# A two-block transformer kernel: the differential stage's first two key units from rows that are not yet scaled, the next two tile by tile, and the weight splits ahead of the rotary operations

## The chip, the cores and the metric

The kernel runs on one core of a Trainium2 chip. The time is the device time of the whole program in microseconds (us), as the median of several runs. The engines of a core work side by side, each through its own queue in order: TensorE (PE in the profile) multiplies, VectorE (DVE), ScalarE (ACT) and GpSimd (POOL) work element by element, SyncE (SP) issues the loads. They wait for one another through semaphores.

## What is computed

Two transformer blocks run over 256 rows of width 1024. The part that matters here is the entry of the second layer of the first block, the differential attention, which needs the keys of the 256 latent rows and of the 256 context rows, and the queries and values of the latent (values also of the context) rows:

```python
def rms_norm(x, gain):
    y = x * lax.rsqrt(jnp.mean(x * x, axis=-1, keepdims=True) + EPS)
    return y * gain
...
h_lat = modulate(rms_norm(x, norm_gain[i, 0]), sh1, sc1)        # h * (1 + scale) + shift
h_ctx = modulate(rms_norm(ctx, norm_gain[i, 0]), csh1, csc1)
...
q, k, v = jnp.split(h @ w_in, 3, axis=-1)
q = rms_norm(q.reshape(b, l, DIFF_HEADS, 2, DIFF_HEAD_DIM), q_gain)
k = rms_norm(k.reshape(b, l, DIFF_HEADS, 2, DIFF_HEAD_DIM), k_gain)
...
q_l = apply_rope(q_l, cos, sin)
k_l = apply_rope(k_l, cos, sin)
```

With g = norm_gain * (1 + scale), a row of h is r * (x * g) + shift, where r is one number for each row (the root of the mean square, inverted). So h @ w is r * ((x * g) @ w) + shift @ w. Before this stage `x` and `ctx` get their last part from the feed-forward layer: x = x + g2 * swiglu(...).

## The kernel before

Everything is held transposed: 128 features on the partitions, rows (512 = 256 latent + 256 context) along the free axis, and a row vector of 1024 features is eight tiles k = 0..7. Each product in 32-bit precision is made of three matmuls (`product`, L514): both operands are split into a rounded half (`wh`, `hh`) and a rest (`wl`, `hl`). ScalarE rounds (`round_half`, L491), VectorE subtracts (`split_low`, L498). Weights come in slabs of two halves; four split halves are held at a time, so half q+4 is rounded and split once half q has been used.

The feed-forward output (`ffn_out`, L2757 on TensorE, L2003 on ScalarE, L2344 on VectorE) ends with eight output tiles in the eight banks of PSUM. VectorE adds each to `x_lat` and `x_ctx` (L2306), ScalarE squares them (`norm_square`, L632), GpSimd adds the first six squares (`squares_added`, L749), and TensorE sums over the features with matrices of ones (`norm_sum`, L758 and L763). Meanwhile TensorE runs 3 and later 9 matmuls that nobody reads (`stay_awake`, L2538). ScalarE makes r from the sum (`norm_rstd`, L642 and L645). Then the rows are scaled tile by tile: VectorE multiplies (L709), ScalarE adds the shift and rounds (L685), VectorE makes the rest (L725); `norm_dve` (L697) and `norm_round` (L675) hold these loops.

`DIFF_UNITS` (L780) lists the stage's work for TensorE: eight key units of 512 columns (one for each pair of 64-wide heads), then four times two query units of 256 columns and four value units ("token"). `units_pe` (L1023) takes the first two units tile by tile as the rows come (each `s_h`), and then one unit after the other. Two places after a head unit (lag 2) follows its `unit_sum` (L986, L987). ScalarE (`units_act`, L1051) squares the unit (L997, L999), makes the inverse root (L1008, L1010) and rounds the next weight half. VectorE (`units_dve`, L1093) scales the unit (L1109, which also frees its bank), turns it (rotary operations, L1124 to L1127), and after these splits the next weight half (L1131).

## Time and profile before

| | |
|---|---|
| median of 3 runs | 1194.3 us (1194.27 to 1195.29) |
| the profiled execution | 1192.11 us, its span 1190.4 us |
| PE busy | 1152.2 us, 97% |
| DVE busy | 732.6 us, 62% |
| ACT busy | 556.2 us, 47% |
| POOL busy | 131.0 us, 11% |
| granted TensorE clock, mean | 0.995 |

The span runs from the first to the last instruction; the time holds about 1.7 us more. A busy PE says little by itself here: the matmuls that keep it awake count as busy, and a matmul's duration overlaps its neighbours', so the distance between the starts of two matmuls is what one costs.

### The profile page before, as it was taken

The page shows a single profiled execution, that of the slowest core. Times are in us where ns is not written, and L with a number is a line of the kernel's source. Part 1 is how long each engine was busy: PE and PEld are TensorE (multiplying, and loading weights), DVE is VectorE, ACT ScalarE, POOL GpSimd, SP SyncE. Part 2 cuts the span into 40 slices and gives each one's busy share as a digit, 9 for nine tenths or more (in the row PEclk, how much of TensorE's full clock was granted, in tenths as well). Part 3 has the DMA queues.
Part 4 walks back from the last instruction along what each step waited for, and adds up shares of the span by engine and source line. Part 5 has one row for each costly group of instructions (what it writes and reads, how often), then busy time and mean ns, then how long its engine had stood idle before and what let it go on. Part 6 is the DMA issues. An engine that isn't in the chain of part 4 may idle for free.

```text
span 1190.4 us, 18791 instructions
## 1 busy us (share of the span) xinstructions
PE 1152.2 (97%) x7072; PEld 963.6 (81%) x7072; DVE 732.6 (62%) x1219; ACT 556.2 (47%) x1058; POOL 131.0 (11%) x185
## 2 busy tenths in 40 slices
PE   8999999999999999999998999999998999999998
PEld 6665787787878888778995799999998986799666
DVE  6764576766723333668769696445568585445773
ACT  4344322222223223455447674444566676467662
POOL 0012011122200000221100110000010010132410
PEclk8999999999999999999999999999999999999999
DMA  8999355578722233122340156555544453164210
GB/s 308 379 338 320 113 168 186 187 246 281 248 98 95 83 106 103 39 91 86 112 138 1 37 177 203 186 176 177 179 150 129 137 160 97 51 202 142 109 72 35
DMA packets 121672, 182.85 MB, mean 154 GB/s; under 512 B 4497, under 2 KB 92896, under 8 KB 121600
## 3 DMA queue, kind: packets, MB, share of 16 engines
q1 hardware_dynamic: 113888, 154.44, 38.9%
q0 software_dynamic: 7712, 27.43, 7.0%
q8 instruction: 47, 0.77, 0.3%
q14 instruction: 25, 0.20, 0.1%
HBM read 180.48 MB, written 1.05 MB: 152 GB/s over the span
## 4 chain that ended last, share of the span: by engine, by line
PE 81%; DVE 9%; ACT 5%; issue 3%; POOL 1%; DVEq 0%; ACTq 0%; POOLq 0%
PE ps L516 20%; PE ps L518 20%; PE ps L517 20%; PE ps L947 2%; DVE wl L498 2%; PE ps L948 2%; PE ps L949 2%; ACT wh L491 1%; PE ps L2563 1%; DVE hl L725 1%; DVE nrm L709 1%; PE ps L2930 1%; PE ps L2932 1%; PE ps L2931 1%; PE ps L1199 1%
## 5 line engine op out<-in xcount | busy, mean ns | idle before, releaser
L498 DVE TENSOR_TENSOR wl<-raw,wh 128x1024 fp32r<-128x1024 f32 (+1 forms) x246 | 297.5, 1214 | 225.7 <-ACT wh L491 222.6
L516 PE MATMUL ps<-hh,wh 128*128 128x256 f32 (+3 forms) x1272 | 418.1, 329 | 7.5 <-DVE hl L725 2.8
L517 PE MATMUL ps<-hl,wh 128*128 128x256 f32 (+3 forms) x1272 | 414.0, 325 | 0.0
L518 PE MATMUL ps<-hh,wl 128*128 128x256 f32 (+3 forms) x1272 | 413.2, 325 | 0.0
L491 ACT ACTIVATE wh<-raw 128x1024 fp32r<-128x1024 f32 (+1 forms) x246 | 252.5, 1032 | 261.1 <-PE ps L518 249.6
L516 PEld LDWEIGHTS ps<-hh,wh 128*128 128x128 f32 x1272 | 239.6, 188 | 47.8 <-issue 14.9
L518 PEld LDWEIGHTS ps<-hh,wl 128*128 128x128 f32 x1272 | 240.0, 189 | 20.9
L517 PEld LDWEIGHTS ps<-hl,wh 128*128 128x128 f32 x1272 | 239.0, 188 | 20.3
L516 PE MATMUL ps<-ah,wh 128*128 128x256 f32 (+2 forms) x376 | 126.1, 335 | 2.7 <-DVE big L1109 1.5
L517 PE MATMUL ps<-al,wh 128*128 128x256 f32 (+2 forms) x376 | 124.2, 330 | 0.0
L518 PE MATMUL ps<-ah,wl 128*128 128x256 f32 (+2 forms) x376 | 124.2, 330 | 0.0
L516 PEld LDWEIGHTS ps<-ah,wh 128*128 128x128 f32 x376 | 70.6, 188 | 11.6 <-DVE big L1109 1.7
L518 PEld LDWEIGHTS ps<-ah,wl 128*128 128x128 f32 x376 | 70.6, 188 | 7.3
L517 PEld LDWEIGHTS ps<-al,wh 128*128 128x128 f32 x376 | 70.8, 188 | 7.1
L2332 DVE TENSOR_TENSOR al<-big,ah 128x512 fp32r<-128x512 f32 (+1 forms) x42 | 23.3, 558 | 81.3 <-ACT ah L1995 81.3
L1995 ACT ACTIVATE ah<-big 128x512 fp32r (+3 forms) x42 | 21.8, 524 | 103.4 <-PE ps L518 103.4
L947 PE MATMUL ps<-wh,hh 128*128 128x256 f32 x192 | 54.8, 286 | 3.2 <-DVE wl L498 1.6
L949 PE MATMUL ps<-wh,hl 128*128 128x256 f32 x192 | 53.9, 281 | 0.0
L948 PE MATMUL ps<-wl,hh 128*128 128x256 f32 x192 | 53.9, 281 | 0.0
L749 POOL TENSOR_TENSOR big<-sq 128x512 f32<-128x512 f32 (+2 forms) x4 | 4.4, 1100 | 441.3 <-ACT sq L632 441.3
L1079 POOL TENSOR_TENSOR al<-sq,ah 128x256 fp32r<-128x256 f32 (+2 forms) x32 | 30.7, 960 | 143.7 <-ACT ah L999 143.7
L1109 DVE SCALAR_TENSOR_TENSOR big<-ps,par,rstd 128x256 f32<-128x256 f32 (+3 forms) x60 | 22.6, 404 | 34.0 <-ACT rstd L1010 33.9
(290 smaller groups left out, 1513.3 us busy)
## 6 DMA issues: line engine op xcount, KB each, us to landing
raw<-in_ffn_w_in SPq DMA_DIRECT2D x44, 1024.0 KB, 5.1
raw<-in_ffn_w_out SPq DMA_DIRECT2D x22, 1024.0 KB, 4.9
raw<-in_w_in SPq DMA_DIRECT2D x22, 1024.0 KB, 5.4
big<-in_w_ada SPq DMA_DIRECT2D x16, 1024.0 KB, 10.5
big<-in_w_ada POOLq DMA_DIRECT2D x24, 512.0 KB, 4.5
ex<-in_w_ada POOLq DMA_DIRECT2D x24, 512.0 KB, 5.1
raw<-in_diff_w_in SPq DMA_DIRECT2D x12, 1024.0 KB, 5.1
raw<-in_w_out SPq DMA_DIRECT2D x8, 1024.0 KB, 4.9
```

Of the source, the lines that this page charges most:

```text
L491: ins = nc.scalar.activation(place(wh), v, ACT.Copy)
L498: ins = nc.vector.tensor_tensor(place(wl), v, place(wh).bitcast(F32), ALU.subtract)
L516: nc.tensor.matmul(o, w_hi, m_hi, start=first, stop=False, **kw)
L517: nc.tensor.matmul(o, w_hi, m_lo, start=False, stop=False, **kw)
L518: return nc.tensor.matmul(o, w_lo, m_hi, start=False, stop=last, **kw)
L947: nc.tensor.matmul(oo, mh[:, k, tok], cols(wh), start=first, stop=False)
L948: nc.tensor.matmul(oo, mh[:, k, tok], cols(wl), start=False, stop=False)
L949: ins = nc.tensor.matmul(oo, ml[:, k, tok], cols(wh), start=False, stop=last)
L1079: nc.gpsimd.tensor_tensor(al[:, h % 2, 0:w], sq[:, h % 2, 0:w], ah[:, h % 2, 0:w].bitcast(F32), ALU.subtract).then_inc(s_ulow, 1)
L1109: ins = nc.vector.scalar_tensor_tensor(out=dst, in0=o[:, a:b], scalar=par_of(u["gain"])[0:m, :], in1=inverse_of(u)[:, a:b], op0=ALU.mult, ...
L1995: nc.scalar.activation(ah[:, at % 2, 0:n], big[:, bass.ds(k * n, n)], ACT.Copy)\
L2332: nc.vector.tensor_tensor(al[:, at % 2, 0:n], big[:, bass.ds(k * n, n)], ah[:, at % 2, 0:n].bitcast(F32), ALU.subtract).then_inc(s_as, 1)
```

## The change

ScalarE and VectorE round and split x * g of each tile (without r) into new tiles `eh` and `el` as soon as the tile is updated, beside the squares. They lie in `big`, which now has a fixed place; behind each part stand two columns with the shift. TensorE starts the first two key units on these tiles right after the feed-forward output, in four banks (256 rows and 2 columns of the shift each), with the sum of the squares behind tile 4; the matmuls that nobody reads fall away here. VectorE scales the two units by r inside the loop over the normed tiles (`first_key_scaled` at k = 3 and 5), ScalarE adds shift @ w and squares them (`first_key_square` at k = 5 and 7). Key units 2 and 3 now take the normed rows tile by tile. Two weight halves are split ahead of r instead of one. The banks of the stage rotate through 5, 6, 0, 1, 2, 3, and the head sums stand in banks 4 and 7. In `units_dve` the weight split stands between the scaling of a unit and its rotary operations.

```diff
+        def key_rows_round(act, k):
+            act.wait_ge(s_x, X_OF["diff"] + k + 1)
+            for x, c, at, w in KEY_PARTS:
+                if k == 0:
+                    nc.scalar.activation(eh[:, :, at + w:at + w + 2], key_shift(c), ACT.Copy)
+                ins = nc.scalar.activation(eh[:, k, at:at + w], x[:, k, :], ACT.Copy, scale=gsc[:, 1, 0, k, c:c + 1])
+            ins.then_inc(s_eh, 1)
+        def key_rows_split(dve, k):
+            dve.wait_ge(s_eh, k + 1)
+            for x, c, at, w in KEY_PARTS:
+                if k == 0:
+                    nc.vector.tensor_tensor(el[:, :, at + w:at + w + 2], key_shift(c),
+                                            eh[:, :, at + w:at + w + 2].bitcast(F32), ALU.subtract)
+                ins = nc.vector.scalar_tensor_tensor(out=el[:, k, at:at + w], in0=x[:, k, :],
+                                                     scalar=gsc[:, 1, 0, k, c:c + 1],
+                                                     in1=eh[:, k, at:at + w].bitcast(F32), op0=ALU.mult,
+                                                     op1=ALU.subtract)
+            ins.then_inc(s_el, 1)
+        def first_key_scaled(dve, j):
+            u = DIFF_UNITS[j]
+            b = u["bank"]
+            unit_done(dve, u)
+            nc.vector.tensor_copy(sml[:, 8 + 2 * j:10 + 2 * j], ps[:, b:b + 2, L:L + 1])
+            for c in range(2):
+                ins = nc.vector.tensor_tensor(first_key(j)[:, c * L:(c + 1) * L], ps[:, b + c, 0:L],
+                                              rstd[:, 0, c * L:(c + 1) * L], ALU.mult)
+            ins.then_inc(s_kt, 1)
+        def first_key_square(act, link, j):
+            act.wait_ge(s_kt, j + 1)
+            for c in range(2):
+                part = first_key(j)[:, c * L:(c + 1) * L]
+                ins = nc.scalar.activation(part, part, ACT.Identity, bias=first_key_bias(j, c))
+            link(ins)
+            nc.scalar.activation(sq[:, j, 0:NT], first_key(j), ACT.Square)
+            nc.scalar.activation(ah[:, j, 0:NT], first_key(j), ACT.Square).then_inc(s_usq, 1)
...
@@ units_dve @@
                     ins.then_inc(s_unrm, 1)
+                if halves and not (i < len(phase) and "early" in phase[i]):
+                    for q in halves_after(phase, i):
+                        split_next(dve, q)
                 if i >= lag and phase[i - lag].get("rope"):
...
-                for q in halves_after(phase, i) if halves else ():
-                    split_next(dve, q)
@@ ffn_out, ScalarE @@
+            def first_keys(k):
+                if k == 5:
+                    first_key_square(act, link, 0)
+                elif k == 6:
+                    unit_done(act, DIFF_UNITS[0])
+                    round_next(act, DIFF_UNITS[0]["q"])
+                elif k == 7:
+                    first_key_square(act, link, 1)
...
+                    else:
+                        key_rows_round(act, m)
                     norm_square(act, norm, m)
-                round_next(act, q0 + 20, 2 if layer == 1 else 1)
+                round_next(act, q0 + 20, 2)
@@ ffn_out, VectorE @@
+            def first_keys(k):
+                if k in (3, 5):
+                    first_key_scaled(dve, (k - 3) // 2)
...
+                    elif layer == 0 and m in (1, 3, 5):
+                        key_rows_split(dve, m // 2)
                 if layer == 0:
-                    split_next(dve, q0 + 20)
+                    for m in range(3, KD):
+                        key_rows_split(dve, m)
+                    split_next(dve, q0 + 20, 2)
                     dve.wait_ge(s_x, X_FFN0 + KD)
-                    norm_dve(dve, norm)
-                    split_next(dve, q0 + 21)
+                    norm_dve(dve, norm, first_keys)
+                    split_next(dve, DIFF_UNITS[0]["q"], 2)
@@ TensorE @@
-                if layer == 0:
-                    pe.wait_ge(s_x, X_OF[norm] + 2)
-                    stay_awake(awake[0], 1, tab, 2 * P)
-                    for k in range(N_ADDED - 1, KD):
-                        norm_sum(pe, norm, k)
-                    stay_awake(awake[1], 7, tab, 2 * P)
...
-            units_pe(pe, DIFF_UNITS[:-1], BASE["diff"])
+            for u in DIFF_UNITS[:2]:
+                unit_start(pe, u, True)
+            for k in range(KD):
+                pe.wait_ge(s_el, k + 1)
+                for u in DIFF_UNITS[:2]:
+                    for _, c, at, w in KEY_PARTS:
+                        n = slice(at, at + w + 2)
+                        ins = product(ps[:, u["bank"] + c, 0:w + 2], tile_of(wh, u["q"], KD, P)[:, k, :],
+                                      tile_of(wl, u["q"], KD, P)[:, k, :], eh[:, k, n], el[:, k, n], k == 0,
+                                      k == KD - 1)
+                    if k == KD - 1:
+                        ins.then_inc(used, 1)
+                if k == 4:
+                    for j in range(N_ADDED - 1, KD):
+                        norm_sum(pe, "diff", j)
+            for u in DIFF_UNITS[2:4]:
+                unit_start(pe, u, True)
+            for k in range(KD):
+                pe.wait_ge(s_h, BASE["diff"] + k + 1)
+                for u in DIFF_UNITS[2:4]:
+                    unit_tile(u, k)
+            units_pe(pe, DIFF_UNITS[:-1], before=4)
```

## Rows read from the trace of the kernel before

**Rows 1.** The page's part 4, the chain that ended last, by engine.
```profile
PE 81%; DVE 9%; ACT 5%; issue 3%; POOL 1%; DVEq 0%; ACTq 0%; POOLq 0%
```

**Rows 2.** Timeline of TensorE, 490 to 502 us: start, duration, what, [idle before, releaser].
```profile
490.68 0.39 PE L518 MATMUL ps<-hh,wl 128*128 128x512 f32 x1
492.84 1.10 PE L758 MATMUL ps<-big,tab 128*128 128x512 f32 x2 [0.48 <-POOL big L749]
493.77 1.88 PE L763 MATMUL ps<-sq,tab 128*128 128x512 f32 x4
495.49 4.05 PE L2538 MATMUL ps<-tab 128*128 128x256 f32 x18
500.08 0.47 PE L516 MATMUL ps<-hh,wh 128*128 128x512 f32 x1 [0.54 <-DVE hl L725]
```

**Rows 3.** The same timeline: the first matmuls of units 2, 3 and 4.
```profile
513.13 0.39 PE L516 MATMUL ps<-hh,wh 128*128 128x512 f32 x1
...
519.16 0.39 PE L516 MATMUL ps<-hh,wh 128*128 128x512 f32 x1
...
525.19 0.39 PE L516 MATMUL ps<-hh,wh 128*128 128x512 f32 x1
```

**Rows 4.** Timelines of ScalarE, VectorE and GpSimd, 483 to 512 us.
```profile
487.12 5.58 POOL L749 TENSOR_TENSOR big<-big,sq 128x512 f32<-128x512 f32 x4 [0.90 <-ACT sq L632]
491.10 0.48 DVE L2306 SCALAR_TENSOR_TENSOR x_lat<-ps,ada,x_lat 128x256 f32<-128x256 f32 x1 [0.49 <-PE ps L518]
495.69 0.69 ACT L642 ACTIVATE rstd<-ps,eps_c 128x512 f32<-128x512 f32 x1 [1.24 <-PE ps L763]
497.13 0.48 DVE L709 SCALAR_TENSOR_TENSOR nrm<-x_lat,gsc,rstd 128x256 f32<-128x256 f32 x1 [1.42 <-ACT rstd L645]
499.05 0.88 DVE L725 SCALAR_TENSOR_TENSOR hl<-nrm,ada,hh 128x256 fp32r<-128x256 f32 x2 [0.25 <-ACT hh L685]
500.77 0.87 DVE L725 SCALAR_TENSOR_TENSOR hl<-nrm,ada,hh 128x256 fp32r<-128x256 f32 x2
500.89 0.91 ACT L685 ACTIVATE hh<-nrm,ada 128x256 fp32r<-128x256 f32 x2 [1.14 <-DVE nrm L709]
```

**Rows 5.** Timelines, the later feed-forward entry (680 to 716 us) and one unit's square.
```profile
696.63 0.28 PE L516 MATMUL ps<-hh,wh 128*128 128x258 f32 x1
...
699.03 0.28 PE L518 MATMUL ps<-hh,wl 128*128 128x258 f32 x1
690.20 0.51 ACT L553 ACTIVATE hh<-x_lat,gsc 128x256 fp32r<-128x256 f32 x1 [0.65 <-DVE x_lat L2306]
690.62 0.40 ACT L632 ACTIVATE sq<-x_lat 128x256 f32<-128x256 f32 x1
...
692.61 0.51 ACT L553 ACTIVATE hh<-x_lat,gsc 128x256 fp32r<-128x256 f32 x1 [0.64 <-DVE x_lat L2306]
693.63 0.95 DVE L563 SCALAR_TENSOR_TENSOR hl<-x_lat,gsc,hh 128x256 fp32r<-128x256 f32 x1
698.43 0.47 DVE L563 SCALAR_TENSOR_TENSOR hl<-x_lat,gsc,hh 128x256 fp32r<-128x256 f32 x1
715.40 0.75 DVE L2472 TENSOR_TENSOR ex<-ps,rstd 128x256 f32<-128x256 f32 x2
512.63 0.60 ACT L997 ACTIVATE sq<-ps 128x512 f32<-128x512 f32 x1 [1.35 <-PE ps L518]
```

**Rows 6.** Timelines around the first value unit and the second slab of values.
```profile
551.82 1.04 ACT L491 ACTIVATE wh<-raw 128x1024 fp32r<-128x1024 f32 x1
555.93 1.22 DVE L498 TENSOR_TENSOR wl<-raw,wh 128x1024 fp32r<-128x1024 f32 x1
557.21 0.39 PE L947 MATMUL ps<-wh,hh 128*128 128x256 f32 x1 [1.10 <-DVE wl L498]
```

**Rows 7.** Two-us windows at 1106 and 1110 us: busy time by engine; the number behind POOL is the granted clock.
```profile
1106.00:1108.00 2.00, 0.97 (x9) 0.57 (x7) 0.23 (x2) 1.19 (x3) 0.00 (x0) 1.00 0.00 0
1110.00:1112.00 2.00, 2.00 (x15) 1.10 (x8) 1.62 (x9) 1.34 (x7) 1.79 (x5) 0.50 0.18 45
```

48 lines of the change are left out of this document (37 added, 11 removed).

## The prediction

> **What bounds the kernel now.** I read the page's shares first, then the chain of waits, then the timeline of each engine through the stage. The chain that ended last lies on TensorE for 81% [rows 1], so a change pays where TensorE has no useful matmul, and only there. The timeline of TensorE shows such a place: the last product of the feed-forward output starts at 490.68 and gives way 0.23 us later, and the first product of the keys starts at 500.08. Between them stand only the sum over the squares (L758 and L763, 492.84 to 495.65) and matmuls that nobody reads [rows 2]. The first two key units then follow the normed rows. VectorE makes one tile in 1.72 us (499.05 to 500.77) [rows 4], while six matmuls cost TensorE 1.39 us: a unit's 24 and a head sum's 2 take 513.13 to 519.16, 0.232 us each [rows 3]. The first pair lasts from 500.08 to 513.13, 13.05 us for 11.1 us of matmuls. Unit 4, the first that both kernels run alike, starts at 525.19 [rows 3]. Its start is my yardstick: behind it TensorE runs closed up until 555.9.
>
> **Part 1: the first pair without the row scale.** It removes the gap and the pacing of the pair. A unit of 512 columns becomes twice 258 columns: the 20 steps from 696.63 to 699.03 take 0.12 us each [rows 5], 12 matmuls in a tile 1.44 us, eight tiles 11.5 us. The sum over the squares stands behind tile 4 and costs what it did, 2.8 us [rows 2], now on TensorE's path. If its operands are there, TensorE runs closed up from 490.9 to 490.9 + 11.5 + 2.8 = 505.2.
>
> Are they there? VectorE adds two tiles (four operations at 0.40, the distance between the L2306 starts) and then splits one, later one after the other; a split is two operations at 0.40 to 0.88 [rows 4, 5]. The last add needs the feed-forward output's last product, as it does now (491.10 [rows 4]). Walking both queues through, with 0.42 us for each of a tile's two roundings (690.20 to 690.62 [rows 5]) and 0.32 for each of its two squares on ScalarE (0.40 long, overlapping as the rounding does), and the upper price wherever GpSimd adds, tile 2 is split at 492.0 (TensorE wants it at 493.8), tile 3 at 494.9 (wanted 495.2), tile 4 at 495.7 (wanted 496.7), tile 7 at 498.0. The eighth square ends near 496.0; TensorE asks for it at 490.9 + 5 x 1.44 = 498.1. So the spare time is 0.3 us at the tightest tile and 2.1 us for the squares. The second price of a split is real: the same operation takes 0.95 us while GpSimd adds and 0.47 when it doesn't [rows 5]. The Trainium skill, "GPSIMD Engine Reference", Key points, says that GpSimd shares its SBUF interfaces with VectorE and collides with instructions that have two SBUF inputs, which these are; the rows agree. If every split paid the upper price, GpSimd adding or not, tile 7 would come at 502.5 instead of 498.0, still ahead of TensorE's 503.8 for it.
>
> **What is late next** is the scale itself. The sum ended at 495.65, now at 498.1 + 2.8 = 500.9. VectorE's first scaling follows 1.44 us later (497.13 after 495.69 [rows 4]), at 502.35 instead of 497.13: this chain starts 5.2 us later than before, and units 2 and 3 hang on it. The second weight split ahead of the scale is hidden: ScalarE has nothing from 498.0 to 500.9, VectorE nothing from 500.4 to 502.35. The half that it makes ready was split after the loop before.
>
> **Part 2: units 2 and 3 tile by tile.** Count from 502.35. The first tile's rest starts at 1.92 (499.05 - 497.13) and further tiles follow at 1.72 [rows 4]. The loop now carries more. On VectorE, each `first_key_scaled` is a copy of two columns and two operations like L2472's (0.75 for two [rows 5]): 0.85 us, on the path at k = 3 and k = 5. On ScalarE, each `first_key_square` is two shifted copies like L685's (0.91 for two [rows 4]), a wait on itself and two squares like L997's (0.60, overlapping to some 0.5 [rows 5]): 2.05 us ahead of tiles 5 and 7; and one rounding (1.04 [rows 6]) ahead of tile 6. ScalarE needs 0.91 of 1.72 us for its own tile. The first square (8.9 to 10.9) delays its tile 5 to 11.8, which VectorE takes only at 12.25; the rounding is hidden too. The second (13.75 to 15.75) isn't: tile 7 is rounded at 16.65 and split at 17.55, where VectorE alone would have been there at 15.8. TensorE ends the second pair 1.39 us after that, at 502.35 + 17.6 + 1.39 = 521.3. The two head sums that stood in the keys' stream before (two matmuls each, 0.46 us) come now: unit 4 starts at 522.2. Its weights are split 1.2 us after VectorE's loop, at 521.1. **Gain: 525.19 - 522.2 = 3.0 us.** The bounds of this term: with ScalarE's second square fully hidden 4.7 us; if the first square too should hold VectorE up, and the roundings with it, 2 us less than 3.0, that is 1.0.
>
> **Part 3: the split ahead of the rotary operations.** In the key stage there's room either way. The place that waits is the first value unit: TensorE is free at 555.93 and starts at 557.21, when VectorE has made a split that began at 555.93, though its rounded half was there at 552.86 [rows 6]. Put ahead of the rotary operations it starts at about 552.9, and 1.28 us fall away. But VectorE has no pause from there to 572.6: four keys' and queries' turns, and then the splits that the next value unit needs. That unit waits now 0.7 us, and its splits would come hardly earlier, since VectorE's work is the same in another order. What isn't lost there is 0 to 1.28 us; I take 0.3. In the latent attention no weight split falls on the same step as a turn, so nothing moves. Turns come 1.2 us later, which only the attention reads, far behind. VectorE starts the key stage with a backlog of some 3 us (units 0 and 1 come with units 2 and 3) and works it off at 1.3 us a unit, just by unit 7.
>
> Banks and the fixed place of `big`: I take nothing. The rotation keeps its depth of six; the first two score steps now need the copies of the last value units, which ScalarE makes in 0.4 us while 2 us of score matmuls run.
>
> **The sum.** 3.0 + 0.3 = 3.3 us. Against the profiled execution: 1192.11 - 3.3 = 1188.8. That execution is 2.2 us faster than the median of the runs, and the forecast is for the median: 1194.3 - 3.3 = **1191.0 us**. About 0.2%, 2.4 us, is what a measurement of this kernel can tell from no change.
>
> **The rivals.**
>
> *Squares late, slower than before.* ScalarE now rounds and squares in one queue, each tile waits for VectorE's adds, which stand behind splits, and for GpSimd's additions. For it: in the later feed-forward entry ScalarE's tiles follow at 2.41 us (690.20 to 692.61 [rows 5]). At that pace from 483.4 the eighth square ends at 503.0, 4.9 us behind TensorE's question; the scale and the second pair move by that, and the time is 1194.3 - 3.3 + 4.9 = 1195.9. It decides when the eighth square ends after 501.4. Against it: those 2.41 us hold a weight rounding of 1.04 and follow TensorE's tiles, and GpSimd's four additions take 5.58 us together [rows 4]. 12 in 100.
>
> *The clock.* The matmuls that nobody reads go. TensorE has work in their place, but in the second pair it stands idle about 1.3 us ahead of each of tiles 5, 6 and 7. The granted clock fell to 0.50 (1.2 GHz of 2.4) at 1110, after two microseconds of which matmuls filled 0.97 [rows 7]. Against it: in the paced pair of before it stayed at 1.00 with 11.1 of 13.05 us filled. At half the clock the last tile costs 1.4 us more and the unit behind it 1 to 2: 1193.5 to 1194.3, say 1193.9. The Trainium skill, "TensorE: Matmul & The Clock Gate", Part 1, says that the half rate is the default and that activity releases it; it speaks against taking such matmuls out, and by it the outcome is this rival's. 10 in 100.
>
> *Given back later, or not taken up.* A wait further on, at the start of the attention or at the value units, or the first pair held back by its tiles, takes the 3 us: 1194. For it: VectorE's backlog meets its busiest stretch. Against it: it's worked off by then, and TensorE's shares behind the stage are high. 12 in 100.
>
> *More than forecast.* ScalarE's squares hide and the split's 1.28 us stay: 4.7 + 1.28 = 6.0, 1188.3. 11 in 100.
>
> **How the numbers follow.** The forecast's case holds 55 in 100, with 1189.5 to 1192.6 as its own range. Faster by over 0.2% (under 1191.9): 0.46 of it and all of the last rival, 0.57. Slower by over 0.2% (above 1196.7 by the bound, the first rival's upper part): with the cases in which the clock and the squares come together, 0.07. The rest, 0.36, is within. The range goes from 1188.5, nearly the last rival's value, to 1194.8, which takes in the clock and the gain given back and leaves the first rival out.
>
> **What would show it.** TensorE's timeline: the first 258-column product at 490.9 (not 492 or later), no idle time over 0.5 us up to 505, the sum's last matmul ending near 500.9. ScalarE: the L642 form at 500.9; eighth square before 498. VectorE: the last normed tile 17.5 us after its first scaling. TensorE's start of unit 4 three microseconds earlier than 525.19. The first value unit right behind its head sum, and the next value unit waiting about as long as the first one gained. Granted clock 1.00 through 490 to 525. The forecast is wrong if the eighth square comes after 498, if the second pair is paced at over 2 us a tile, or if the start of the attention isn't earlier by what unit 4 was.

## The result, and the profile after

| | before | after |
|---|---|---|
| median of 22 runs each, on one chip | 1194.48 us | 1196.81 us |
| the profiled execution | 1192.11 us | 1196.62 us |
| its span | 1190.4 us | 1194.8 us |
| DVE busy | 732.6 us | 747.2 us |
| granted TensorE clock, mean | 0.995 | 0.995 |

The ratio after/before is 1.0022, 95% interval 1.0016 to 1.0028: the changed kernel is **slower by 2.3 us**, where 1191.0 was forecast and 1188.5 to 1194.8 was the range. Of the 4.5 us between the two profiled executions, 1.5 lie in the start-up (the last product of the feed-forward output starts at 492.22 instead of 490.68); every time of after below is 1.5 us late for that reason, and "shifted" means with 1.5 taken off. The other 3.0 lie in the stage of the change.

The chain that ended last (the page's part 4, by engine) shows TensorE's share fallen from 81% to 78% and VectorE's risen from 9% to 12% [rows 1]:

```profile
PE 78%; DVE 12%; ACT 5%; issue 4%; DVEq 0%; POOL 0%; ACTq 0%; POOLq 0%
```

TensorE's timeline of after (start, duration, what, [idle before, releaser]), from the sum over the squares to the second slab of values:

```profile
500.70 1.88 PE L829 MATMUL ps<-sq,tab 128*128 128x512 f32 x4
502.02 0.69 PE L525 MATMUL ps<-eh,wh 128*128 128x258 f32 x1
...
517.63 0.50 PE L525 MATMUL ps<-hh,wh 128*128 128x512 f32 x1 [1.60 <-DVE hl L791]
...
521.81 0.50 PE L525 MATMUL ps<-hh,wh 128*128 128x512 f32 x1 [0.82 <-DVE hl L791]
...
524.24 0.39 PE L525 MATMUL ps<-hh,wh 128*128 128x512 f32 x1
...
556.60 0.38 PE L1023 MATMUL ps<-wh,hh 128*128 128x256 f32 x1 [1.44 <-DVE wl L507]
...
569.47 0.36 PE L525 MATMUL ps<-hh,wh 128*128 128x256 f32 x1 [0.78 <-DVE nrm L1187]
...
578.54 0.39 PE L1023 MATMUL ps<-wh,hh 128*128 128x256 f32 x1 [2.90 <-DVE wl L507]
```

Against [rows 3] and [rows 6], shifted: unit 4 starts 2.45 us earlier than before (522.74 against 525.19), the first value unit still 2.1 us earlier (555.1 against 557.21). The value unit at 578.54 belongs to the second slab. Before, it started at 575.51, so it is now 1.5 us later. That is where the sign turns: TensorE waits 2.9 us for VectorE's weight split. And right behind this wait the granted clock (the number behind POOL) falls to 0.50, that is 1.2 of 2.4 GHz, though TensorE is full. In these windows of after:

```profile
576.00:578.00 2.00, 0.00 (x0) 0.00 (x0) 2.00 (x2) 1.28 (x3) 0.99 (x1) 1.00 0.00 0
578.00:580.00 2.00, 1.46 (x10) 1.46 (x11) 2.00 (x3) 0.00 (x0) 0.00 (x0) 0.86 0.19 31
580.00:582.00 2.00, 2.00 (x11) 2.00 (x10) 0.76 (x1) 0.00 (x0) 0.00 (x0) 0.50 0.95 328
582.00:584.00 2.00, 2.00 (x15) 2.00 (x15) 0.00 (x0) 0.78 (x3) 0.00 (x0) 0.78 1.10 361
584.00:586.00 2.00, 2.00 (x19) 2.00 (x19) 1.48 (x4) 0.39 (x1) 0.00 (x0) 1.00 1.00 325
```

The three windows of 2 us at 0.86, 0.50 and 0.78 cost 0.3 + 1.0 + 0.4 = 1.7 us of work. From 590 us on after is some 3 us behind before (shifted), and stays there to the end. The mean clock hides this: before has a fall of the same size at 1110 us [rows 7] that after hasn't, but there it moves its end by under 0.2 us, since TensorE isn't what that stretch waits for. By the Trainium skill, "TensorE: Matmul & The Clock Gate", Part 1, it is activity that holds the full rate; the rows agree so far that the clock falls behind the wait of 2.9 us and stays at 1.00 behind those of 1.60 and 1.44.

VectorE's and ScalarE's timelines of after tell why VectorE is late: ScalarE's square of unit 2 (L1073) stands in its queue ahead of unit 0's inverse (L1086), and waits for TensorE. VectorE scales unit 0 at 526.46, shifted 3.2 us later than before (521.78):

```profile
524.03 0.60 ACT L1073 ACTIVATE sq<-ps 128x512 f32<-128x512 f32 x1 [2.57 <-PE ps L1063]
525.73 0.63 ACT L1086 ACTIVATE rstd<-rstd 128x512 f32<-128x512 f32 x1
526.46 0.49 DVE L1187 SCALAR_TENSOR_TENSOR big<-ex,par,rstd 128x256 f32<-128x256 f32 x1 [2.44 <-ACT rstd L1086]
```

And why it stays late: GpSimd's subtraction on the squares (L1157) and VectorE's rotary operations (L1205, four for each unit) now fall together. Both engines' timelines of after:

```profile
543.58 1.22 DVE L507 TENSOR_TENSOR wl<-raw,wh 128x1024 fp32r<-128x1024 f32 x1
543.77 2.17 POOL L1157 TENSOR_TENSOR al<-sq,ah 128x512 fp32r<-128x512 f32 x1 [4.69 <-ACT ah L1075]
544.82 2.75 DVE L1205 TENSOR_TENSOR big<-nrm,tab 32x256 f32<-32x256 f32 x4
549.80 1.75 POOL L1157 TENSOR_TENSOR al<-sq,ah 128x512 fp32r<-128x512 f32 x1 [3.86 <-ACT ah L1075]
550.43 3.27 DVE L1205 TENSOR_TENSOR big<-nrm,tab 32x256 f32<-32x256 f32 x4
```

The same in the groups by line and form of VectorE, 475 to 580 us (busy, mean ns of one | idle before). First before, where all meetings but one (a group of 2.25 us at 552.85) are missing because VectorE pauses 9.9 us in all for ScalarE's inverse and GpSimd works in these pauses; then after:

```profile
L1124 DVE TENSOR_TENSOR big<-nrm,tab 32x256 f32<-32x256 f32 x40 | 17.2, 429 | 1.3
L1109 DVE SCALAR_TENSOR_TENSOR big<-ps,par,rstd 128x256 f32<-128x256 f32 x8 | 3.9, 483 | 9.9 <-ACT rstd L1010 9.9
```

```profile
L1205 DVE TENSOR_TENSOR big<-nrm,tab 32x256 f32<-32x256 f32 x40 | 21.1, 528 | 1.2
L1187 DVE SCALAR_TENSOR_TENSOR big<-ps,par,rstd 128x256 f32<-128x256 f32 x6 | 2.9, 478 | 0.0
```

### The profile page after: what moved, and what is told of

The parts are those of the page before. It is cut to its first block, busy times and chain, and to the rows that moved or that the text cites. A ratio compares the mean times of both kernels' runs of the same rounds, so it can differ in the third digit from the quotient of the medians.

```text
span 1194.8 us, 18887 instructions
## 1 busy us (share of the span) xinstructions
PE 1149.9 (96%) x7096; PEld 963.6 (81%) x7096; DVE 747.2 (63%) x1243; ACT 563.6 (47%) x1080; POOL 131.4 (11%) x185
## 4 chain that ended last, share of the span: by engine, by line
PE 78%; DVE 12%; ACT 5%; issue 4%; DVEq 0%; POOL 0%; ACTq 0%; POOLq 0%
PE ps L525 19%; PE ps L526 19%; PE ps L527 19%; DVE wl L507 3%; PE ps L1023 2%; PE ps L1024 2%; PE ps L1025 2%; DVE big L1205 2%; PE ps L2663 1%; ACT wh L500 1%; DVE hl L791 1%; DVE nrm L775 1%; PE ps L3045 1%; PE ps L3047 1%; PE ps L3046 1%
## 5 line engine op out<-in xcount | busy, mean ns | idle before, releaser
L525 PE MATMUL ps<-hh,wh 128*128 128x256 f32 (+3 forms) x1256 | 412.2, 328 | 10.7 <-DVE hl L791 5.3
L526 PE MATMUL ps<-hl,wh 128*128 128x256 f32 (+3 forms) x1256 | 407.7, 325 | 0.0
L527 PE MATMUL ps<-hh,wl 128*128 128x256 f32 (+3 forms) x1256 | 406.8, 324 | 0.0
L525 PEld LDWEIGHTS ps<-hh,wh 128*128 128x128 f32 x1256 | 236.6, 188 | 50.9 <-issue 15.5
L527 PEld LDWEIGHTS ps<-hh,wl 128*128 128x128 f32 x1256 | 237.0, 189 | 20.3
L526 PEld LDWEIGHTS ps<-hl,wh 128*128 128x128 f32 x1256 | 236.0, 188 | 19.5
L1157 POOL TENSOR_TENSOR al<-sq,ah 128x256 fp32r<-128x256 f32 (+2 forms) x32 | 31.0, 970 | 144.5 <-ACT ah L1075 122.1
L1144 ACT ACTIVATE big<-ps 128x256 f32<-128x256 f32 x48 | 18.4, 382 | 54.9 <-PE ps L1025 42.8
```

Of the source, the lines that this page charges most:

```text
L525: nc.tensor.matmul(o, w_hi, m_hi, start=first, stop=False, **kw)
L526: nc.tensor.matmul(o, w_hi, m_lo, start=False, stop=False, **kw)
L527: return nc.tensor.matmul(o, w_lo, m_hi, start=False, stop=last, **kw)
L1157: nc.gpsimd.tensor_tensor(al[:, h % 2, 0:w], sq[:, h % 2, 0:w], ah[:, h % 2, 0:w].bitcast(F32), ALU.subtract).then_inc(s_ulow, 1)
```

## The experiments

Eighteen kernels ran in five groups; each group has its own runs of the kernel before on the same chip. Seventeen stand in the table; the eighteenth came out as a plain repeat of before and is told in the text. Differences below are against these; where a time is set beside after's 1196.81 us, that one is from another group.

The last column comes from the profiled execution of each kernel, one for each: the time from the last product of the feed-forward output (490.68 in before [rows 2]) to the operation that is at 715.40 in before [rows 5], less the 224.7 us that this takes in before. It leaves out the start-up and all that lies behind the stage. By it after is 3.0 us slower.

| kernel | us | before in its group | ratio (95% interval) | stage in its trace, us |
|---|---|---|---|---|
| order undone in after | 1196.87 | 1194.26 | 1.0023 (1.0014 to 1.0031) | +3.2 |
| order alone in before | 1194.26 | 1194.26 | 1.0001 (0.9992 to 1.0010) | 0.0 |
| fixed place alone in before | 1194.33 | 1194.26 | 1.0003 (0.9994 to 1.0011) | 0.0 |
| subtraction on 2 columns, after | 1189.99 | 1194.26 | 0.9967 (0.9955 to 0.9979) | -4.1 |
| the same, before | 1193.54 | 1194.45 | 0.9989 (0.9978 to 1.0000) | -0.9 |
| the same, after, key units 0 to 5 only | 1194.28 | 1193.95 | 1.0001 (0.9991 to 1.0012) | +0.1 |
| early head sums, after | 1196.51 | 1194.45 | 1.0016 (1.0005 to 1.0027) | +1.0 |
| the same with the order undone | 1196.83 | 1194.45 | 1.0015 (1.0006 to 1.0024) | +2.8 |
| VectorE started late, before | 1196.66 | 1193.95 | 1.0022 (1.0013 to 1.0031) | +1.6 |
| subtraction on VectorE, last, after | 1199.55 | 1193.95 | 1.0052 (1.0034 to 1.0070) | +4.4 |
| the same, before | 1196.89 | 1193.95 | 1.0025 (1.0014 to 1.0037) | +3.0 |
| subtraction on VectorE, first, after | 1197.46 | 1193.84 | 1.0018 (1.0004 to 1.0033) | +2.5 |
| the same with early head sums | 1195.59 | 1193.84 | 1.0018 (1.0009 to 1.0027) | +0.5 |
| the same (without the sums), before | 1193.84 | 1193.84 | 1.0001 (0.9992 to 1.0010) | -0.1 |
| slab's splits first, after | 1192.73 | 1194.17 | 0.9996 (0.9987 to 1.0005) | -2.5 |
| the same, before | 1194.17 | 1194.17 | 0.9997 (0.9988 to 1.0006) | -1.5 |
| all three edits, after | 1190.58 | 1194.17 | 0.9966 (0.9955 to 0.9978) | -4.8 |

The two measures part where the clock falls outside the stage. At 920 us of before TensorE waits 2.25 us for ScalarE, and in all twenty profiles it waits as long there. In six of them the granted clock falls behind this wait, as in "VectorE started late" here, and 1.3 to 1.5 us are lost; in the other fourteen, before and after among them, it stays at 1.00.

```profile
923.57 0.36 PE L516 MATMUL ps<-hh,wh 128*128 128x256 f32 x1 [2.24 <-ACT big L1066]
```

```profile
924.00:926.00 2.00, 2.00 (x12) 2.00 (x11) 1.53 (x2) 2.00 (x5) 0.00 (x0) 0.50 0.87 330
```

The six are the early head sums, the late start, the subtraction last (after), the subtraction first with the sums, and the slab's splits first in both kernels. In each of them the median stands 1.0 to 1.5 us worse against its before than the stage does, so a median near before's doesn't say for them that the stage is as long as before's.

### The parts that cost nothing

First theory: the new order (part 3) sends the rotary operations into GpSimd's time, and the loss is its. In after the order is put back, in before it is put in:

```diff
                     ins.then_inc(s_unrm, 1)
-                if halves and not (i < len(phase) and "early" in phase[i]):
-                    for q in halves_after(phase, i):
-                        split_next(dve, q)
                 if i >= lag and phase[i - lag].get("rope"):
...
                     meta_summed(dve, link, phase[i])
+                if halves and not (i < len(phase) and "early" in phase[i]):
+                    for q in halves_after(phase, i):
+                        split_next(dve, q)
```

> The changed kernel with one part undone: in the unit loop of VectorE the weight split stands behind the rotary operations again. Theory of the collision: after the change the rotary operations of the key units fall on the time in which GpSimd makes the rest of the squares (a group of four took 2.75 and 3.27 us instead of 1.76), VectorE never works off its lateness, and the value units wait for weight splits (2.89 us at 575.4). With the old order VectorE catches up, the 2.6 us won at unit 4 stay: 1192 us. Rival, lateness alone: VectorE starts the key units 3 us later against TensorE whatever the order, the second value unit waits as long, 1196 to 1197 us. Rival, other places (banks, the fixed place of the big tile): 1196 to 1197 us too.

> The kernel before with only the order in VectorE's unit loop changed: weight split ahead of the rotary operations. Theory of the collision as an effect of lateness and order together: without lateness the rotary operations of a unit would end at about 526.5, just ahead of GpSimd's operation at 526.6, so they hardly meet: 1194 to 1195 us, the first value unit's wait of 1.28 us gone and most of it back at the second one. If the order costs by itself: 1196 to 1197.5 us. If the order is a plain gain: 1193.2 us.

1196.87 against 1196.81, and 1194.26 against 1194.26: the theory fell in this form, and part 3 gives nothing either. What it does is move the wait. In the kernel before the first slab's 1.10 us go and the second slab's 0.53 become 1.94:

```profile
575.88 0.39 PE L947 MATMUL ps<-wh,hh 128*128 128x256 f32 x1 [1.94 <-DVE wl L498]
```

TensorE of after with the order undone, and its windows there (the clock's number behind POOL again):

```profile
559.59 0.58 PE L1023 MATMUL ps<-wh,hh 128*128 128x256 f32 x1 [4.46 <-DVE wl L507]
```

```profile
556.00:560.00 4.00, 0.41 (x2) 0.41 (x3) 3.87 (x8) 2.04 (x3) 0.76 (x1) 0.86 0.00 0
560.00:564.00 4.00, 4.00 (x20) 4.00 (x20) 3.81 (x8) 0.00 (x0) 0.00 (x0) 0.50 0.78 261
```

One wait of 4.45 us at the first slab in place of 1.44, 0.78 and 2.90 at three places: 5.1 us in all, and a fall of the clock behind the longest of them in both. In these two orders VectorE's lateness is paid once, wherever its queue meets a split that TensorE wants.

The fixed place of `big` was the other suspect, for the start-up:

```diff
-        big = sb("big", [P, 13824])
+        big = nc.alloc_sbuf_tensor_at("big", [P, 13824], F32, offset=174048)
```

> The kernel before with the big tile at the fixed place of the changed kernel, nothing else. Rival of the place: the profile of the changed kernel was 1.5 us late by 30 us from the start, where nothing of the change runs; if the place did it, 1196 us. Theory of the collision, and start-up scatter: 1194.5 us, as before.

1194.33: nothing. The 1.5 us of the start-up are scatter between executions: in the profiles of the kernels that are like before up to this stage the start-up is 0.1 to 2.6 us longer than in before's.

### The meeting with GpSimd

```diff
-                    h, w = u["h"], u["w"]
+                    h, w = u["h"], 2 if phase is DIFF_UNITS else u["w"]
```

> The changed kernel with GpSimd's operation on the squares of the differential units cut to 2 columns of 512 or 256 (the rest of the squares is left as it was in the tile, so the head sums are less exact). Theory of the collision: with nothing to meet, each group of rotary operations is back at 1.76 us, VectorE has caught up by unit 7, the value units wait at most 1 us: 1192 us. Rival, lateness alone: nothing changes, 1196 to 1197 us.

> The kernel before, in which GpSimd's subtraction on the squares of the differential stage works on 2 columns instead of 256 or 512, so that the rest of the squares is left out of their sums. It is the control for the same cut in the kernel after, which made that one 6.8 us faster. Theory 1 (the cut helped because VectorE's work of the kernel after meets GpSimd's; in the kernel before, the subtractions fall into VectorE's idle time ahead of each unit's scaling, 526.61 to 527.90 beside VectorE's pause from 526.50 to 527.81): no more than the one group that meets it now (552.85, 2.25 instead of 1.76 us) and the waits of the value slabs, 1193.3 to 1194.3 us. Theory 2 (the subtraction, or the wait for it in the head sums, lies on the path of both kernels): a gain like the 6.8 us of the kernel after, 1187.5 to 1189 us.

After falls to 1189.99 (by 6.8 us; 7.1 in the stage of the traces), before only to 1193.54 (0.9 in both). So the subtraction isn't dear by itself or by TensorE's wait for it, it is dear beside the VectorE of after. The narrow form of after shows the stage as the prediction had it. VectorE's group of rotary operations, and VectorE catching up by unit 5, where it waits again (the first such wait since unit 0):

```profile
L1205 DVE TENSOR_TENSOR big<-nrm,tab 32x256 f32<-32x256 f32 x44 | 18.4, 417 | 1.4
```

```profile
550.77 0.48 DVE L1187 SCALAR_TENSOR_TENSOR big<-ps,par,rstd 128x256 f32<-128x256 f32 x1 [1.15 <-ACT rstd L1086]
```

Without meetings its units follow at 4.63 us beside TensorE's 6.03; in after at 6.75, 4.63, 4.95, 5.61, 6.14.

Is lateness enough to set the meetings off? In the kernel before, seven more scalings of unit 0's first half start VectorE 3.6 us late, with nothing else changed. (A first attempt at this, by a condition that never held, left the program as it was: 1194.46 against 1194.45, a plain repeat of before.)

```diff
+                    for _ in range(7 if phase[0] is DIFF_UNITS[0] and u["h"] == 0 else 0):
+                        link(nc.vector.scalar_tensor_tensor(
+                            out=outs[0][0], in0=o[:, outs[0][1]:outs[0][2]], scalar=par_of(u["gain"])[0:m, :],
+                            in1=inverse_of(u)[:, outs[0][1]:outs[0][2]], op0=ALU.mult, op1=ALU.mult))
```

> The kernel before, in which VectorE makes the first half of the scaling of the first key unit seven more times, one waiting for the other (the same values in the same place; about 3.4 us), so that its work starts the key stage that much later; nothing else is changed. Theory 1 (a late VectorE meets GpSimd's subtractions, which follow TensorE's pace of 6.03 us, and each meeting costs VectorE 1.0 to 1.5 us, as much as the 1.3 us that it could work off in a unit): the rotary groups take 2.2 to 3.3 us instead of 1.76, VectorE's scalings are 2 to 4 us late up to the sixth unit, the first slab of values waits longer, 1196 to 1199 us. Rival (lateness alone): worked off at 1.3 us a unit by the third or fourth unit, groups at 1.76 us, no wait of TensorE is longer, 1194.0 to 1194.8 us.

1196.66: 2.7 us slower (1.6 to 3.7 by the interval), from 3.6 us on an engine that paused 9.9 us in this stage. In its trace the stage is 1.6 us longer; that execution lost another 1.5 to the fall of the clock at 924 us, which isn't the mechanism looked for here. GpSimd and VectorE in it:

```profile
528.01 1.29 POOL L1079 TENSOR_TENSOR al<-sq,ah 128x512 fp32r<-128x512 f32 x1 [4.74 <-ACT ah L999]
527.73 2.76 DVE L1128 TENSOR_TENSOR big<-nrm,tab 32x256 f32<-32x256 f32 x4
...
534.05 1.32 POOL L1079 TENSOR_TENSOR al<-sq,ah 128x512 fp32r<-128x512 f32 x1 [4.75 <-ACT ah L999]
533.36 2.75 DVE L1128 TENSOR_TENSOR big<-nrm,tab 32x256 f32<-32x256 f32 x4
...
560.22 0.39 PE L947 MATMUL ps<-wh,hh 128*128 128x256 f32 x1 [2.72 <-DVE wl L498]
```

Each of five units pays 1.0 us (2.76 for 1.76 in the first three, an operation of 1.4 for 0.42 in the others), so VectorE works off 0.4 us a unit instead of 1.3, is still 1.6 us late at unit 5 (554.94, with 1.4 of start-up taken off, against 551.94), and the first slab waits 2.7 instead of 1.1 us [rows 6]. This carries the mechanism over to a kernel that has none of the change.

Where in the stage is the loss made? The cut for key units 0 to 5 only:

```diff
+                    h, w = u["h"], 2 if phase is DIFF_UNITS and u["h"] < 6 else u["w"]
```

> The kernel after, in which GpSimd's subtraction works on 2 columns for the first six key units only (the rest of their squares is left out of the sums) and in full for the last two key units and the queries. It tells where in the stage the loss is made. Theory 1 (the meetings in the key units keep VectorE late, and what it meets later is like before): nearly all of the 6.8 us that the cut in the whole stage gave, 1190 to 1191.5 us. Rival (the meetings in the busiest stretch, from 550 us on, make it): 1194 to 1196.5 us.

1194.28, which neither side had: 2.5 us of the 6.8. With that cut VectorE comes to unit 5 3.5 us earlier than in after (549.54 against 553.04, shifted each by its own start-up) and the second slab starts 2.9 us earlier (574.1 against 577.0), yet TensorE still waits 2.91 us for it and its clock falls (0.68 in 576 to 580 us). The next groups are about this.

### An earlier start, and the subtraction on VectorE

TensorE makes the sums of units 0 and 1 behind tiles 6 and 7, ScalarE makes unit 0's inverse inside the loop:

```diff
                 for u in DIFF_UNITS[2:4]:
                     unit_tile(u, k)
+                if k >= 6:
+                    unit_sum(pe, DIFF_UNITS[k - 6])
...
+                    unit_inverse(act, link, DIFF_UNITS[0])
                     round_next(act, DIFF_UNITS[1]["q"])
```

> The kernel after, in which TensorE makes the head sums of the first two key units behind tiles 6 and 7 of the second pair, where it waits for VectorE anyway, and ScalarE makes the inverse root of unit 0 inside the loop over the tiles, ahead of the square of unit 2. Unit 0's scaling on VectorE then isn't held by ScalarE's wait for unit 2 (it started at 526.46 after 2.44 us without work) and starts near 524.0. Theory 1 (lateness that meets GpSimd's subtractions makes the loss): VectorE is 2.4 us earlier, the lateness is worked off before the value units, most of the loss goes: 1190.5 to 1193.5 us. Rival (the loss has nothing to do with when VectorE starts the key stage): 1196 to 1197 us, less the 0.46 us by which TensorE's two sums now fill idle time.

> The same early sums as in the run above, with the weight splits back behind the rotary operations. With the two orders equal in the kernel after (1196.87 against 1196.81 us), Theory 1: the same as the run above within 1 us, now by the 0 to 1.3 us that the order was meant to give at the first slab of values. If the order mattered once the lateness is gone, this one is slower by up to 1.3 us.

1196.51 and 1196.83: next to nothing by the medians. VectorE did start 1.5 us earlier, straight into GpSimd's subtraction: that scaling took 1.52 instead of 0.48 us and the split behind it 2.32 instead of 1.22. The first expectation was missed; the two came within 1 us of one another, as the second said. Most of an earlier start is lost as long as the meeting stands: the second slab starts 0.4 us earlier than in after.

The first of these traces also holds what no run was made for. TensorE waits 2.88 us for the second slab there too, and by chance the clock stays at 1.00 behind it:

```profile
579.11 0.39 PE L1023 MATMUL ps<-wh,hh 128*128 128x256 f32 x1 [2.88 <-DVE wl L507]
```

```profile
580.00:584.00 4.00, 4.00 (x36) 4.00 (x35) 1.81 (x3) 1.17 (x3) 0.00 (x0) 1.00 0.98 314
```

Its stage is 2.0 us shorter than after's, and 0.4 of that stand at the slab already. The other 1.5 us are what the fall costs after, near the 1.7 read from the windows, though by one execution of each kernel only.

So the subtraction goes to VectorE itself (0.68 us for 512 columns), behind the rotary operations of its step:

```diff
+                if i < len(phase) and "low" in phase[i] and phase[0] is DIFF_UNITS[0]:
+                    h, w = phase[i]["h"], phase[i]["w"]
+                    dve.wait_ge(s_usq, h + 1)
+                    nc.vector.tensor_tensor(al[:, h % 2, 0:w], sq[:, h % 2, 0:w], ah[:, h % 2, 0:w].bitcast(F32),
+                                            ALU.subtract).then_inc(s_ulow, 1)
```

> The kernel after, complete, but the subtraction on the squares of the differential stage (10 of them) is made by VectorE, behind the rotary operations of the same step, instead of by GpSimd. By the weight split of 1024 columns (1.22 us) one of 512 costs VectorE about 0.65 us. Theory 1 (each of GpSimd's subtractions costs a busy VectorE 1.0 to 1.5 us): VectorE gains 0.4 to 0.9 us a unit against the kernel after, all rotary groups at 1.76 us, the long wait of the value slabs (2.89 us) and the fall of the granted clock behind it (0.71 in 580 to 585 us) go: 1190.5 to 1193.5 us, faster than both kernels. Rival (only the missing work made the narrow form fast): VectorE has more work of its own in the stage, 1196 to 1199 us.

> The control for the run above: the same move of the subtraction to VectorE in the kernel before, where GpSimd's subtractions fall into VectorE's pauses. Theory 1: nothing is won, VectorE's work beside the value slabs grows by 0.4 us for each query unit, 1194.3 to 1196 us. Rival (GpSimd's subtraction is dear in both kernels, because the head sums wait for it): 1191 to 1193 us.

1199.55 and 1196.89: the worst of all, and a plain miss. The meetings are gone (all groups at 1.76 us), but now TensorE's head sums wait for what stands last in VectorE's step, five times between 1.2 and 1.85 us. One of them:

```profile
558.98 0.50 PE L1062 MATMUL ps<-ah,half_r 128*128 128x512 f32 x1 [1.84 <-DVE al L1213]
```

Hence the same for key units 2 to 7 alone, as the first work of the step, without and with the early sums, and its control:

```diff
             for i in range(len(phase) + lag):
+                if phase[0] is DIFF_UNITS[0] and i < len(phase) and 2 <= phase[i].get("h", 0) < 8:
+                    h, w = phase[i]["h"], phase[i]["w"]
+                    dve.wait_ge(s_usq, h + 1)
+                    nc.vector.tensor_tensor(al[:, h % 2, 0:w], sq[:, h % 2, 0:w], ah[:, h % 2, 0:w].bitcast(F32),
+                                            ALU.subtract).then_inc(s_vlow, 1)
                 if i >= lag and phase[i - lag]["kind"] == "head":
```

> The kernel after, complete, with the subtraction on the squares of key units 2 to 7 on VectorE, now as the first work of its step (0.68 us each, by the run with it behind the rotary operations, where TensorE's head sums waited 1.2 to 1.8 us for it five times); those of units 0 and 1 and of the queries stay on GpSimd. Theory 1 (a meeting costs VectorE 1.0 us or more in each key unit, its own subtraction 0.68 us, and its place in the queue made the loss of the run before): VectorE works off about 0.75 us in each unit instead of 0.1 to 0.4, no head sum waits over 0.5 us, 1192 to 1194.5 us. Rival (the move doesn't pay wherever it stands, because VectorE bounds the stage and has no more room than before): 1195.5 to 1199 us.

> The run above together with the early head sums of units 0 and 1, so that VectorE's first scaling isn't held by ScalarE's wait for unit 2 and what it gains isn't eaten by a meeting (there its scaling at 526.01 took 1.52 instead of 0.48 us and its weight split 2.32 instead of 1.22). Theory 1: 0.5 to 1.5 us less than the run above, 1191 to 1193.5 us, under both kernels. Rival: no difference between the two.

> The control: the same move (key units 2 to 7, first in the step) in the kernel before, where GpSimd's subtractions fall into VectorE's pauses. Theory 1: VectorE's pauses take the 0.68 us in, 1193.3 to 1194.8 us, no gain beyond the one meeting at 552.85 us. Rival (the move itself is a gain in either kernel): 1191 to 1193 us.

1197.46, 1195.59 and 1193.84. The waits of the head sums are gone, the control gains nothing as expected, but after gains nothing clear of noise either: another miss. (The twelve executions of the first fall apart: four at 1192.3 to 1193.0, eight at 1196.2 to 1199.0. Only one of the eight was profiled, so what parts them stays open.) VectorE comes to unit 5 1.8 and 2.8 us earlier than in after (shifted), and the second slab starts 1.8 and 2.5 us earlier, but TensorE still waits as long for it and the clock falls behind the wait, in the first form for 3.4 us of work instead of 1.7. In the form without the early sums:

```profile
576.78 0.58 PE L1024 MATMUL ps<-wh,hh 128*128 128x256 f32 x1 [2.90 <-DVE wl L508]
```

Five kernels with different histories wait 2.88 to 2.92 us there. TensorE can't bring a lead of its own to this place: it starts the third query on the bank that VectorE's scaling of the first one frees (0.3 to 0.8 us of wait there). From that scaling the two run in step. TensorE has two query units and is done 6.8 us after its start. VectorE has two turns of 2.65 us, the second with a meeting, and the splits, and brings the slab 9.7 us after it (568.84 to 578.54 in after, 567.07 to 576.78 here).

### The slab's splits first

Second theory: this order is what decides. As soon as the last value unit is done, ScalarE rounds and VectorE splits both halves of the next slab, and VectorE turns the second query behind them. In the control the slab's two splits, which stood behind the rotary operations there, move ahead of them too:

```diff
         def halves_after(phase, i):
+            if phase[0] is DIFF_UNITS[0]:
+                u = phase[i] if i < len(phase) else {"frees": 0}
+                return list(range(u["q"] + 1 - u["frees"], u["q"] + 1)) if u["frees"] else []
...
-                if i >= lag and phase[i - lag].get("rope"):
-                    u = phase[i - lag]
+                turned_now = [phase[i - lag]] if i >= lag and phase[i - lag].get("rope") else []
+                if phase[0] is DIFF_UNITS[0] and turned_now and i + 2 < len(phase) and phase[i + 2]["frees"] == 2:
+                    turned_now = []
+                if phase[0] is DIFF_UNITS[0] and i < len(phase) and phase[i]["frees"] == 2:
+                    turned_now = [phase[i - 4]]
+                for u in turned_now:
```

> The kernel after, complete and with GpSimd's subtraction where it was, in which the two halves of the next slab of values are rounded and split as soon as the last value unit is done, and VectorE turns the second query of the pair only behind these splits (2.65 us of rotary operations that TensorE doesn't wait for). In the kernel after the slab's splits stand behind them, at 575.60, and TensorE waits 2.89 us; in the runs with less work in the key units it waits 2.90 us again. Theory 2 (VectorE's order ahead of the second slab is what loses, 2.9 us of waiting and some 1.7 us of the lower granted clock right behind it, 0.71 in 580 to 585 us): no wait and no fall of the clock there, 1191.5 to 1193.5 us, faster than both. Rival (the wait only moves to the next place at which VectorE is late): 1195 to 1197 us.

> The control: the same order in the kernel before, where TensorE waits 0.53 us for the second slab and the clock doesn't fall. Theory 2: a gain of at most 0.5 us, 1193.3 to 1194.3 us. Rival (the order is a gain of its own in either kernel): 1191 to 1192.5 us.

> The kernel after with the splits of the slab first, the subtractions of key units 2 to 7 first in VectorE's step, and the early head sums. With the second slab's wait gone, what VectorE wins in the key units counts. Theory 2: 0.5 to 1.5 us less than after_slab_first, 1190.5 to 1192.5 us. Rival: the same as that run, since VectorE's lateness in the key units is hidden once the slab's splits come early.

By the medians the first two came as theory 2 had it, and the third in its range, though by 2.2 us under the first where 0.5 to 1.5 were expected. After goes to 1192.73, the control stays at 1194.17. The traces say more: after's stage gets 5.5 us shorter (from +3.0 to -2.5), and the control's, too, gets 1.5 us shorter, in small steps at three slabs. That lies just past the end of the interval of its median (1.4 us faster to 0.7 slower), and its profiled execution lost 1.3 of it to the clock at 922 us. So the larger part of the gain belongs to the kernel after, but that the order gives nothing on the kernel before isn't shown. VectorE of after with this order, and the window of 5 us behind it:

```profile
571.40 0.48 DVE L1190 SCALAR_TENSOR_TENSOR nrm<-ps,par,rstd 128x256 f32<-128x256 f32 x1
571.79 2.89 DVE L507 TENSOR_TENSOR wl<-raw,wh 128x1024 fp32r<-128x1024 f32 x2
574.72 2.20 DVE L1212 TENSOR_TENSOR big<-nrm,tab 32x256 f32<-32x256 f32 x4
```

```profile
575.00:580.00 5.00, 5.00 (x45) 5.00 (x44) 4.84 (x8) 2.77 (x6) 0.79 (x1) 1.00 0.65 213
```

TensorE doesn't wait for the slab at all, the clock stays at 1.00 where it fell, and the time falls by 3.8 us by the medians, 3.1 by the ratios to before (from 1.0022 to 0.9996; the interval, 0.9987 to 1.0005, doesn't show a gain on that kernel for certain). With the slab out of the way the key units count: all three edits together give **1190.58 us**, 3.6 us under the kernel before, with none of the slab waits left.

What is the change itself worth once VectorE is out of its way? Two pairs answer. With the subtraction on 2 columns after is 3.4 us better than before, each against its own group (3.2 in the traces); that is about what was forecast, on kernels that leave part of the work out. With the slab's splits first it is 1.4 us by the medians and 1.0 in the traces. For all three edits together no partner ran on the kernel before, so how much of their 3.6 us is the change's isn't shown.

## Why the prediction was wrong, step by step

- **Part 1 held.** TensorE's first pair ran closed up: no idle time over 0.15 us from 490 to 512. The eighth square started at 496.92, shifted 495.4, ahead of 498.1. The sum's inverse (L708) came at 502.62, shifted 501.1 against 500.9; the first scaling at 504.06, shifted 502.55 against 502.35. The two prices of a split were there (0.47, and 1.11 to 1.51 beside GpSimd). The rival of the late squares didn't occur.
- **Part 2 held, a little short.** The last tile started at 521.81, shifted 520.3; with the two head sums behind it unit 4 at 522.74 instead of 522.2. The gain is 2.45 for 3.0. One scaling inside the loop met GpSimd (1.43 instead of 0.48 us), and so did the last split (1.14 for 0.88).
- **The upper bound of part 2** was worked out wrong. It sets 17.55, the end of the last split, against 15.8, where VectorE alone would have started it. Start against start the second square costs 16.65 less 15.8, 0.85 us, so the bound is 3.9 us and not 4.7, and the rival "more than forecast" stood at 1189.2. The trace has the start at 16.55, and VectorE ready for it 1.33 us before.
- **The first failed step** is part 3's sentence that VectorE starts the key stage "with a backlog of some 3 us" and "works it off at 1.3 us a unit, just by unit 7". The backlog was sized right (3.2 us). The rate was not: it took VectorE's durations from a stretch in which GpSimd worked in VectorE's pauses, and a late VectorE has no pauses. From unit 0 to unit 5 it took 28.1 us, where five units without meetings take 23.2: it worked off 2.1 us, 0.4 a unit, and was 1.1 us later than before at unit 5 (553.04 against 551.94), where TensorE was over 2 us earlier. (Taken alone, 3 us at 1.3 us a unit would be gone by the third unit; unit 7 fits only if the 3 us that TensorE gains are to be made good too.) The prediction had this price in part 1 for the splits and didn't carry it to the rotary operations.
- **The second failed step** is the yardstick: that what unit 4 gains reaches the end. Behind 552 us VectorE has no pause, and the start of each slab of values is its own, not TensorE's. The prediction said "That unit waits now 0.7 us, and its splits would come hardly earlier", and drew the conclusion for part 3's 1.28 us only, not for the 3.0 us of part 2.
- **The rival "given back later, or not taken up"** named the place ("VectorE's backlog meets its busiest stretch") at 12 in 100 and at no loss. It was taken as a floor at the time of before. But VectorE arrived later than before in absolute terms (1.5 us at the second slab), and a wait of 2.9 us costs more than itself.
- **The clock's rival** was right in kind and wrong in place. Nothing fell in the entry, where matmuls that nobody reads were taken out and waits of 1.6 us stand (1.00 through 490 to 560). It fell behind the 2.9 us wait at 576, and cost 1.5 to 1.7 us.
- **Part 3 and the banks** came out at 0: the order moved one wait of 4.45 us into three of 5.1 in all. The wait of 0.78 us at the third query is for the bank that the first query's scaling frees. The kernel before has the same two queries in one bank, six units apart, so it is VectorE's lateness that shows there; no run changed the banks alone.

The loss in the trace adds up: 2.45 us gained at unit 4. Against that, 0.35 lost at the first slab's wait (1.44 for 1.10), 0.95 up to the third query, 2.7 up to the second slab (wait of 2.9 for 0.5), 1.6 behind it by the clock: some 3 us lost in these profiled executions. The medians are 2.3 apart; the rest is scatter between executions, in the start-up and in the clock. What the clock alone costs was not tested by an edit (no run filled the wait with matmuls that nobody reads); it is read from the windows, from the 1.6 us by which after falls back behind them, and from the one trace with the same wait and no fall.

## What to carry to other kernels

A gain on the bounding engine lasts to the next place that another engine sets. Walk the second-busiest engine from the edit to its next stretch without pauses, and ask whether it too gets there earlier; if it starts later, its durations must be taken as they are beside everything that used to work in its pauses. And where such an engine feeds the bounding one, the order inside its queue (what is waited for first, what nobody waits for last) was worth more here than the edit itself: 3.8 us by the medians and 5.5 in the stage of the traces, against 0 and 1.5 in the kernel whose VectorE was on time.

## What the runs showed of the hardware

- **GpSimd's and VectorE's operations hold one another up.** With GpSimd's subtraction (1.29 us alone) under way a group of four rotary operations of 1.76 us takes 2.75, a scaling of 0.48 takes 1.43 to 1.52, a split of 1.22 takes 2.32. In turn GpSimd's takes 2.17 when it is issued 0.2 us after VectorE's split of 1.22 has begun (543.77 beside 543.58). This agrees with the Trainium skill, "SBUF — State Buffer", section "SBUF: two separate sides", by which the shared pair of ports is held by one of the two for a whole instruction and the other blocks. The operations met here were on 32 and 128 partitions, all with two inputs in SBUF.
- **The meetings keep themselves up.** Against 1.3 us of spare time in a unit, 1.0 us a meeting leaves 0.3 to 0.4 us: of 3.6 us of lateness in the kernel before 1.6 were left five units later, where 1.3 a unit would have cleared them in three. They cost 1.6 us in the stage of the trace, 2.7 by the medians.
- **Behind a wait of 2 to 4.5 us TensorE can run at 1.2 GHz for some microseconds, and the length of the wait alone doesn't decide it.** Of the seven kernels with a wait of 2.88 to 4.46 us at a slab, six show a fall behind it (0.50 to 0.68 in a window of 4 us; 1.7 or 3.4 us of work in all); in the one with the early head sums the clock stayed at 1.00 behind 2.88 us. Behind the slab wait of 2.72 us it stayed. Behind the wait of 2.25 us at 920 it fell in six profiles and stayed in fourteen. A fall costs only where TensorE is what the stretch waits for: 1.6 us at 580 us, 1.3 to 1.5 at 920 to 930, under 0.2 at 1110.
